# Two-block fp32 network on one core: second layer's heads rotated and turned between the column blocks of its projections, cosine tables scaled by the gains, routed layer's opening in another order

## What is computed

```
p_lat = h_lat @ w_in                       # 256 x 2304: 8+8 query heads, k, v
p_ctx = h_ctx @ w_in[:, OD_Q:]             # 256 x 1280: k, v only
def rms_norm(x, g): return x * rsqrt(mean(x*x) + eps) * g      # over each head's 64 elements
cq, dq, ck, dk (latent) = apply_rope(rms_norm(., gain))        # rotated by position
ck, dk (context)        = rms_norm(., gain)                    # not rotated
y = merge(window_gqa(cq, ck, cv, ...), diff_attention(dq, dk, dv, ...)) @ w_out
h = h + g1 * y
logits = norm(h) @ router; the best 2 of 8 experts for each token, softmax of their logits
h = h + g2 * sum_e gate_e * swiglu_e(norm(h))
```

## Time and profile before

| | |
|---|---|
| median of 3 runs | 3195.71 us (3195.0 to 3195.91) |
| the profiled execution, own time | 3196.73 us |
| span in its profile | 3194.9 us |
| PE busy | 2826.9 us (88% of the span) |
| DVE, ACT, POOL busy | 1831.3, 1522.7, 147.1 us |
| mean granted clock of PE | 0.930 |

### The profile page before, as it was taken

The page is one execution under the profiler, slowest core; times in us unless marked ns, Lnnn a source line. Parts: engine busy times, 40 slices in busy tenths (PEclk is TensorE's granted clock), DMA queues, the critical chain, the costliest instruction groups (busy, mean ns, idle before and its releaser), DMA issues.

```text
span 3194.9 us, 34582 instructions
## 1 busy us (share of the span) xinstructions
PE 2826.9 (88%) x13343; PEld 2335.9 (73%) x13343; DVE 1831.3 (57%) x2220; ACT 1522.7 (48%) x2142; POOL 147.1 (5%) x195
## 2 busy tenths in 40 slices
PE   6897689989975877999999899898689989897798
PEld 5775578878864556888888688677578878787587
DVE  5566556656646444555688755447655555545555
ACT  4553245545534323444677644463444444445344
POOL 1012000000011000000000000000100000100000
PEclk8998889999987786999999999899799999999899
DMA  7662146656662003555799845450045545560354
GB/s 254 230 223 72 53 143 226 211 172 220 214 137 92 1 1 125 178 170 170 238 321 330 292 158 182 135 186 12 7 148 166 193 164 177 182 197 17 99 159 143
DMA packets 266417, 511.15 MB, mean 160 GB/s; under 512 B 9252, under 2 KB 40188, under 8 KB 266267
## 3 DMA queue, kind: packets, MB, share of 16 engines
q1 hardware_dynamic: 262320, 498.11, 46.8%
q0 software_dynamic: 3952, 11.07, 1.7%
HBM read 508.05 MB, written 1.05 MB: 159 GB/s over the span
## 4 chain that ended last, share of the span: by engine, by line
PE 80%; DVE 9%; ACT 5%; DMA 3%; issue 2%; POOL 2%; DVEq 0%; ACTq 0%; POOLq 0%; SPq 0%
PE bank L377 22%; PE bank L378 22%; PE bank L381 21%; PE bank L1061 2%; PE bank L1074 2%; DVE wlo L325 2%; PE bank L2030 2%; ACT whi L321 1%; PE bank L1087 1%; PE bank L746 1%; PE bank L1699 1%; DMA raw<-in_od_w_in 1%; PE bank L465 1%; DMA raw<-in_moe_w 1%; PE bank L1736 1%
## 5 line engine op out<-in xcount | busy, mean ns | idle before, releaser
L325 DVE TENSOR_TENSOR wlo<-raw,whi 128x1024 fp32r<-128x1024 f32 (+1 forms) x1012 | 1196.8, 1199 | 910.6 <-ACT whi L321 906.2
L321 ACT ACTIVATE whi<-raw 128x1024 fp32r<-128x1024 f32 (+1 forms) x1012 | 1037.5, 1039 | 902.4 <-PE bank L381 860.5
L377 PE MATMUL bank<-whi,xhi 128*128 128x512 f32 (+2 forms) x2432 | 935.8, 385 | 36.8 <-DVE wlo L325 17.3
L378 PE MATMUL bank<-wlo,xhi 128*128 128x512 f32 (+2 forms) x2432 | 925.8, 381 | 0.0
L381 PE MATMUL bank<-whi,xlo 128*128 128x512 f32 (+2 forms) x2432 | 924.8, 380 | 0.0
L377 PEld LDWEIGHTS bank<-whi,xhi 128*128 128x128 f32 x2432 | 465.5, 191 | 130.2 <-issue 41.3
L381 PEld LDWEIGHTS bank<-whi,xlo 128*128 128x128 f32 x2432 | 464.5, 191 | 83.0
L378 PEld LDWEIGHTS bank<-wlo,xhi 128*128 128x128 f32 x2432 | 465.8, 192 | 79.8
L377 PE MATMUL bank<-whi,f_hhi 128*128 128x512 f32 x528 | 210.3, 398 | 3.1 <-ACT f_gates L781 3.1
L378 PE MATMUL bank<-wlo,f_hhi 128*128 128x512 f32 x528 | 209.3, 396 | 0.0
L381 PE MATMUL bank<-whi,f_hlo 128*128 128x512 f32 x528 | 209.2, 396 | 0.0
(11 more groups left out here) (449 smaller groups left out, 2692.0 us busy)
## 6 DMA issues: line engine op xcount, KB each, us to landing
raw<-in_ffn_w SPq DMA_DIRECT2D x180, 1024.0 KB, 5.1
raw<-in_moe_w SPq DMA_DIRECT2D x96, 1024.0 KB, 6.0
raw<-in_ada_w SPq DMA_DIRECT2D x48, 1024.0 KB, 5.9
raw<-in_moe_w SPq DMA_DIRECT2D x48, 768.0 KB, 4.6
raw<-in_ev_w_in SPq DMA_DIRECT2D x24, 1024.0 KB, 6.1
raw<-in_ffn_w SPq DMA_DIRECT2D x36, 512.0 KB, 3.6
raw<-in_hyb_w_in SPq DMA_DIRECT2D x18, 1024.0 KB, 5.0
raw<-in_attn_w_qkv SPq DMA_DIRECT2D x18, 1024.0 KB, 5.1
```

Source lines behind the costliest of these rows:

```text
L321: nc.scalar.activation(whole, part, ACT.Copy).then_inc(sem("w_hi"), 1)
L325: nc.vector.tensor_tensor(wlo[s][:, 0:rows, 0:n], part, whole.bitcast(F32), ALU.subtract)\
L377: nc.tensor.matmul(bank[:, 0:n], xk_h, whi[s][:, wk, 0:n], start=first, stop=False)
L378: ins = nc.tensor.matmul(bank[:, 0:n], xk_h, wlo[s][:, wk, 0:n], start=False, stop=last and xl is None)
```

## The change

The cosine and sine tables are multiplied by the gains once, on POOL (`gcos`, `gsin`), after each gain is loaded as one row of 64 to all partitions. On DVE a head is then rotated first, without its root (`odd_products_dve`, `odd_turn_dve`), and multiplied by its root afterwards (`odd_scaled_dve`); the two keys of the window attention are written twice over (`odd_twins_dve`), so that one transpose gives both halves. The steps are spread over both projections: queries in the latent one, keys in the context's. PE turns the queries after the first and second block of the context projection. The context's roots come from ACT (Sqrt) and a reciprocal on DVE. In the routed layer the logits go tile by tile, the rows' low parts are made before the weights, expert 0's rows are gathered in one go into eight banks, and the transposes of its selection move into the first expert's stream.

```diff
-        for name, hd, n in (("od_cq_g", 0, 8), ("od_dq_g", 8, 8), ("od_ck_g", 16, 2), ("od_dk_g", 20, 8)):
-            side_load(e, gain[:, hd * HD:(hd + n) * HD].rearrange("p (h d) -> p h d", h=n),
-                      a[name].rearrange("o (h d) -> o h d", h=1).broadcast_to([P, n, HD]), "odd")
+        for g, name in enumerate(("od_cq_g", "od_dq_g", "od_ck_g", "od_dk_g")):
+            side_load(e, gain[:, g, :], a[name].broadcast_to([P, HD]), "odd")
...
+        for t in range(NT):
+            e.link(nc.gpsimd.tensor_tensor(gcos[:, t, :, :], gain[:, :, :], cos.broadcast_to([P, 4, HD]), ALU.mult))
+            for b in range(2):
+                e.link(nc.gpsimd.tensor_tensor(quarters(gsin[:, t, :, :])[:, :, :, b, :],
...
+    def odd_q_dve(e, i, outs):
+        if i == 4:
+            e.after("odd tables")
+            e.eng.wait_ge(sem("out_done"), outs + 2)
+            odd_products_dve(e, 0, Q_PARTS)
+        if i == 5:
+            for t in range(NT):
+                odd_sums_dve(e, t, 16, 0, SS_Q, f"sq_q{t}", "ss_q")
+            odd_turn_dve(e, 0, 0, 16)
+        if i == 6:
+            odd_products_dve(e, 1, Q_PARTS)
+        if i == 7:
+            odd_turn_dve(e, 1, 0, 16)
+        if i in (8, 9):
+            t = i - 8
+            e.after("q_o:root")
+            odd_scaled_dve(e, pl, t, 0, 16, SS_Q + 16 * t, f"q_o{t}")
+        if i == 9:
+            for t in range(NT):
+                odd_sums_dve(e, t, 12, OQ, SS_L, f"sq_k{t}", "ss_l")
...
+    def odd_k_dve(e, i, outs):
+        if i in (0, 1):
+            odd_products_dve(e, i, K_PARTS)
+            for hd, n, _ in K_PARTS:
+                odd_turn_dve(e, i, hd, n)
+        if i in (2, 3):
+            odd_twins_dve(e, pl, t, 16, c, twin_lat, None)
+            odd_scaled_dve(e, pl, t, 20, 8, c + 4, "k_lat")
+        if i == 3:
+            lambda_dve(e)
...
-        e.after("moe:xf7")
-        for t in range(NT):
-            for k in range(KD):
+        for k in range(KD):
+            e.after(f"moe:xf{k}")
+            for t in range(NT):
...
-        e.after("rows_lo")
-        select_pe(e, 0)
-        e.after("selT0")
-        gather_pe(e, 0, 0)
-        e.after("moe_x00")
-        gather_pe(e, 0, 1)
+        e.after("sel0", "rows_lo")
+        for r, banks in enumerate(FIRST_BANKS):
+            gather_pe(e, 0, r, banks)
...
+                root_pool(e, "q_o", SS_Q, SS_Q + 32, HD, "ss_q")
+                root_pool(e, "k_o", SS_L, SS_L + 24, HD, "ss_l")
                 norm_pool(e, "in_o1")
-                odd_roots_pool(e)
```

More of the change, by code:

```diff
@@ L1448, in odd_lat_dve @@
[L1448 to L1461, removed]
+        quarters = lambda ap: ap.rearrange("p g (a b c) -> p g a b c", a=2, b=2)
@@ new lines, in odd_k_act @@
+    def odd_k_act(e, i, outs):
+        if i == 1:
+            e.after("odd loads")
+            e.put(nc.scalar.activation(unit_[:, :], ident, ACT.Copy))
+            e.link(nc.scalar.activation(band[:, :, :].rearrange("p t k -> p (t k)"), kTo[:, 0, :], ACT.Copy), "band")
+        if i == 4:
+            e.eng.wait_ge(sem("out_done"), outs + 2)
+            e.after("q_o1")
+            for t in range(NT):
+                e.put(nc.scalar.activation(sq[:, t, 0:768], pc[:, t, 0:768], ACT.Square), f"sq_c{t}")
+        if i in (2, 4):
+            e.after(f"qoT_ps{i // 4}")
+            for b in range(2):
+                k = i // 4 * 4 + 2 * b
+                e.put(nc.scalar.activation(qTo[:, k:k + 2, :].rearrange("p k t -> p (k t)"), T[b][:, :], ACT.Copy),
+                      f"qoT{i // 4}")
+        if i == 4:
+            e.after("ss_c")
+            e.put(nc.scalar.activation(ss[:, SS_C:SS_C + 24], ss[:, SS_C:SS_C + 24], ACT.Sqrt, scale=1.0 / HD,
+                                       bias=epsc[:, 0:1]), "std_c")
@@ new lines, in odd_k_out, with odd_k_take @@
+    def odd_k_out(e):
+        e.after("ckT_ps")
+        for b in range(2):
+            e.put(nc.scalar.activation(kTo[:, b, :], psum[b][:, :], ACT.Copy), "ckT")
+        e.after("dkT_ps0")
+        e.put(nc.scalar.activation(kTo[:, 2, :], psum[2][:, :], ACT.Copy), "dkT0")
+        e.after("lam dots")
+        e.link(nc.scalar.activation(lame[:, 2:4], lame[:, 0:2], ACT.Exp), "lam exp")
+    def odd_k_take(e):
+        for b in (1, 2, 3):
+            e.after(f"dkT_ps{b}")
+            e.put(nc.vector.tensor_copy(kTo[:, 2 + b, :], psum[2 + b][:, :]), "dkT")
@@ L1702, in gather_pe, with first_gather_act @@
         e.put(ins, f"moe_ps{i}{r}")
+    def first_gather_act(e):
+        for r, banks in enumerate(FIRST_BANKS):
+            e.after(f"moe_ps0{r}")
+            for j in range(2):
+                k0 = 4 * r + 2 * j
+                e.put(nc.scalar.activation(xhi[:, k0:k0 + 2, :], banks[j][:, :].rearrange("p (k t) -> p k t", k=2),
+                                           ACT.Copy), f"moe_x0{r}")
     def gather_act(e, i, r):
@@ L1782, in experts_pe @@
                         scatter_pe(e, i - 1)
-                else:
+                    else:
+                        select_pe(e, 0)
+                else:
+                    if j == 1 and i == 0:
+                        e.after("selT0")
                     if j == 1 and 1 <= i <= 3:
```

271 lines of the change are left out of this document (140 added, 131 removed).

## The result

| | before | after |
|---|---|---|
| median of 4 runs | 3195.81 us (3195.0 to 3199.14) | 3145.86 us (3140.23 to 3153.41) |
| the profiled execution, own time | 3196.73 us | 3141.8 us |
| its span | 3194.9 us | 3140.0 us |
| mean granted clock of PE | 0.930 | 0.938 |

The ratio is 0.984, 95% interval 0.982 to 0.986: some 50 us faster, 3 us more than forecast. Runs of the changed kernel lie 13 us apart, and the profiled one is among the fastest of them. Five more runs of it gave a median of 3150.6 (3144.4 to 3154.7) with the before kernel at 3196.6 beside them, ratio 0.9845 (0.9831 to 0.9858). Each stretch begins at an instruction that both have: PE's first latent product, its first context product, the attention's first product, DVE's first step of the routed layer's norm, PE's first expert product; the rest ends with DVE's last operation.

What follows compares the result with a forecast made beforehand. PE bounds most stages (busy 88% of the span), but three stretches hold 72 us of idle PE. Gains of 36.3 + 10.4 = 46.7 us from 3196.73 give 3150.0, median 3149.0 us; range 3144 to 3154 (0.66).

Steps and rivals of the forecast that it cites:

- Step 1: Latent projection: with fewer gain rows the weight unit's stall goes and the last block leaves the banks 11.5 us earlier.
- the gap at 939: Latent projection: PE's wait for a late weight unit, until 948.31 before; forecast to disappear.
- The first rival: Latent projection: router or a fixed time per load sets the landing, the stall stays; 3161.6 us, 12.6 more; chance 0.07.
- my range for them: Small loads at the latent projection: all twelve down between 926.4 and 934.3.
- The tables: DVE's list in the latent projection: waiting for `gcos` and `gsin` makes the kernel slower than before; chance 0.02.
- Step 2: Handover from latent to context projection: DVE's list and POOL's roots give back most of 11.5 us, 1.0 left.
- Step 3: Tail from context projection to attention: attention starts at 1020.4, not 1056.7; gain 36.3 us with Step 2's 1.0.
- the Sqrt: Tail ahead of the attention: ACT's root of the context, given no time, up to 1.5 us possible.
- Step 4: Routed layer's opening: first expert product 11.7 us earlier, 1.3 given back inside the stream, net 10.4 us.
- The rival of late weights: Routed opening: the expert's first two weight units come only as late as before; 3158 us; chance 0.09.
- The rule weighed: Two-input DVE operations and GpSimd reads of SBUF exclude each other; queries' roots would hold DVE for their whole length.
- the third rival: POOL holds DVE: the queries' 6 us of roots go onto DVE's list; 3155 us; chance 0.07.

Runs made afterwards that it cites:

- e5: Kernel before with only the gains loaded compactly (512 rows, not 3328) and written out for the heads by POOL; 3184.0 us, ratio 0.9952.
- e4: Changed kernel with the gains loaded as before, 3328 rows of 256 bytes, still twelve loads; 3162.9 us, ratio 0.9896.
- e1: The changed kernel again, no edit; 3150.6 us (3144.4 to 3154.7), ratio 0.9845 to the kernel before.
- e2: Changed kernel with POOL computing the context norm's roots ahead of the latent keys' roots; 3147.9 us, ratio 0.9844.
- e3: e2 with DVE's sums of the latent keys' squares also moved behind the context's norm; 3137.0 us, ratio 0.9804.
- e9: e3 with the queries' two scalings also moved behind the context's norm; 3147.4 us, ratio 0.9845.
- e6: Kernel before with only the routed layer's opening changed to the new one; 3189.8 us, ratio 0.9969.
- e7: Changed kernel with the routed layer's opening of before; 3158.4 us, ratio 0.9874.
- e11: Changed kernel with the logits in the old order, waiting for all eight tiles first; 3147.4 us, ratio 0.9846.
- e10: e3 with PE computing products nobody reads in the gaps around the routed opening; 3130.4 us, ratio 0.9785.
- e8: e3 with PE computing 29 products nobody reads in the gaps ahead of the attention; 3132.3 us, ratio 0.9787.

## Why the prediction held

**Step 1, the small loads: right.** The weight unit lands in 5.2 us, all loads were down by 919.9, the gap at 939 is gone. e5 alone gives 13.2 us, 11.4 without its faster start, where 11.5 stood. e4 gives it back. The first rival, that the router or the number of loads sets the time, falls: e4 changes rows only. The twelve loads landed earlier than my range for them: the 11.2 us that I gave the other 1664 rows are not their price, since the router is down 6.5 us after its issue now. The tables never held DVE. The same rival's 12.6 us stand in no row: by the earlier trace rows it was 11.5, and with the old rows back e4 took 14.7.

**Step 2, the handover: right in mechanism, 0.5 to 2.3 us too dear.** DVE's list without a hole, then POOL with the keys' roots first, is what the rows show. The list from block 3's copy took 24.5 us (936.75 to 961.24) where I had 25.1 (939.4 to 964.5). The block itself came 2.6 earlier: 0.8 because the first latent product did, 1.8 because the projection's first products ran fast in that execution. By the stretch 3.3 us were left and not 1.0; in e1, where those products were slow as before, it was 1.5. So all but 0.5 of the miss is the clock at the start. e2 and e3 are the proof: each operation taken out of the way ahead of the norm came back as time, 5.65 and 2.0. e9 shows where that ends.

**Step 3, the tail: right, 1.9 us too long.** From PE's last context product to the attention 13.3 us passed, 13.5 were forecast; the twins took 0.44 each, the Sqrt waited for nothing on the path. The 1.9 is the context's start: I kept the slow first products of before (0.77, 0.63), and they ran at 0.47 and 0.40. My terms behind DVE's list add up to 1020.1 and not to 1020.4; that changes nothing.

**Step 4, the opening: right, its net by two misses that cancel.** 12.7 us measured in e1, e6 and e7 where 11.7 stood, 16.5 in the first profile. e11 prices the logits' order at 3.1 (I had 2.5). The selection inside the stream took 1.2 (I had 1.3), but the first expert's products ran slow for longer, which I had at nothing and which cost another 1.2. Net it is 10.3 where 10.4 stood. The rival of late weights falls: the last gap waits for DVE's split.

**What the sum did not have.** The attention gave back 2.7 us in the first profile and 4.5 in e1: I had it unchanged. The earlier trace rows are of a PE that came to it at a granted clock of 1.00, and now it comes at 0.50. In e1 all of the 4.5 are there at the sixth pair of scores, which starts 19.1 us after the first and not 14.6; in the first profile 1.7 of the 2.7 are.

**How much of the number is luck.** Against the forecast the four stretches are off by -2.3, -1.9, +2.7 and -4.8 us in the first profile, by -0.5, -1.9, +4.5 and -0.9 in e1; the rest by -1.1 and +2.1. The mechanisms held, but the misses have both signs, and most of them follow PE's clock, which I did not forecast. That they cancelled to 3 us in the first four runs is luck: the nine runs of this program lie between 3140.2 and 3154.7, with a median of 3149.9.

**The rule weighed.** POOL's power over 32 columns ran for 6.44 us beside DVE's splits and six of its products, all at their usual lengths. The rule of the Trainium skill (SBUF — State Buffer, Who interferes with whom) would have held DVE for those 6 us; the trace doesn't agree, and the third rival falls. POOL did pay. Its scaling of 32 columns (942.58) took 1.18 us beside DVE's turn of 1.22, that of 24 columns, with DVE idle, 0.21; the power took 6.44 where 24 columns took 4.17, which would make 5.6 for 32. This lay off the path here.

## What to carry to other kernels

Count the rows of a small load, not its bytes (256 KB in 128 rows landed in 3.0 us, in 1024 rows in 14.6 and more): a broadcast written out per head took 11 us from a stream of weights that had nothing to do with it. When work is moved into the shadow of another engine, look at what stands at the next handover; an in-order queue gives the gain back there, and the order of two short operations on a third engine can be worth 5.65 us. Moving too much behind the handover costs more than it won (e9: 2.0 won, 9.0 lost beside the slow first products), so a list is shortened until the next engine waits and no further.

## What the runs showed of the hardware

TensorE's granted clock moves such a kernel by several us from one execution to the next. The same program took 34.1 us for the opening in one execution and 30.2 in another, with mean granted clocks of 0.55 and 0.67 there, where 0.50 is the level of 1.2 GHz and 1.00 that of 2.4 (table of stretches of e1 and of the first profile):

```profile
1166.80:1200.90 34.10, 22.65 (x106) 21.92 (x107) 18.07 (x62) 11.24 (x22) 0.73 (x2) 0.55 0.35 123
```

With products that nobody reads it was 0.88 and 28.7 us (the same of e10):

```profile
1150.40:1179.10 28.70, 25.35 (x145) 22.12 (x145) 17.90 (x62) 11.24 (x22) 0.74 (x2) 0.88 0.36 128
```

Such filling paid there, where short steps follow a gap for 30 us: 5.4 us in the stretch and 2.8 behind it. At the attention the profiles show no gain: with filling the granted clock was 0.93 in its first 4 us (e8) and 0.50 in the next 4, with PE busy. The kernel before did the same with no filling, 0.75 and then 0.50. No kernel here changes anything ahead of the first latent product, and in the profiles it still fell between 896.8 and 905.9 us; so a difference of a few us is read from a stretch between two instructions, and only then from medians.
